# Strassen block products of four feed-forward stages: another order of weight roundings, sums and first pair on each engine, a fourth raw weight buffer, and rests at stretch ends on GpSimd

## The chip, the cores and the metric

The kernel runs on one core of a Trainium2 chip. The metric is the device time of one execution in microseconds (us). Engines are named as in the profile: PE is TensorE, DVE is VectorE, ACT is ScalarE, POOL is GpSimd, SP is SyncE (it issues the weight transfers).

## The reference

Two transformer layers with a context stream come first (neighbourhood attention, differential attention, a convolution branch), then two "macaron" layers on 512 positions of width 1024. Each of those has two feed-forward stages, so there are four:

```
def macaron_layer(x, mixer, ...):
    x = x + FFN_HALF * rmsnorm(swiglu(rmsnorm(x, ffn1_pre_g), ffn1_w_in, ffn1_w_out), ffn1_post_g)
    x = x + rmsnorm(mixer(rmsnorm(x, mix_pre_g)), mix_post_g)
    x = x + FFN_HALF * rmsnorm(swiglu(rmsnorm(x, ffn2_pre_g), ffn2_w_in, ffn2_w_out), ffn2_post_g)
    return x
```

`swiglu` multiplies by `w_in` (1024 by 5632: 2816 gate and 2816 up columns), takes silu(gate) * up, and multiplies by `w_out` (2816 by 1024). All is fp32.

## The kernel before

**Three products for one.** Every fp32 weight piece w is split into hi (rounded to the PE's fp32r format by ACT, line 390) and lo = w - hi (a subtraction on POOL or DVE, line 405 for whole pieces, 410 and 416 for others). The activations are split in the same way. PE then makes hi*hi + hi*lo + lo*hi (`mm3`).

**Units.** A feed-forward stage has 22 tiles of 128 hidden columns, each with a gate piece and an up piece of `w_in` (512 KB each). Tiles 0, 1 and 2 ("direct") are multiplied plainly. Each tile u from 3 to 21 is a *unit*: gate and up together are one 2 by 2 block product made with seven block products in Winograd's form of Strassen's scheme. The operands are quarters of the gate and up pieces ("plain"), four weight sums, and four combinations t0 to t3 of the activations. The weight sums are made by POOL: s1 and s2 (lines 425 and 427, together the entry "s12"), s3 and s4 (lines 429 and 431, "s34"). ACT rounds them (line 390), DVE makes their lo (line 416). The second half of the up piece is the entry "last" (lo at line 410 on DVE). A unit on PE is, in this order, the products p1, p2 (plain), p5, p6 (s12), then p4 of the unit before (its "last"), then p7, p3 (s34). Each product is 4 x 3 matmuls of 128x256, so a unit is 84.

**What is done with the products.** ACT copies p1 out of PSUM (line 1449); p6 of the same unit is added to the same bank, and so waits for that copy. ACT copies U2 = p1 + p6 (line 1456). DVE makes c11 (1582), u4 (1588), c22 (1597), c12 (1555, `gate_dve`) and c21 (1564, `up_dve`), scales gate and up by the norm (1502, twice), multiplies (1508), and makes the lo of the result (1513). ACT makes silu (1416) and the hi of the result (1423).

**Phases.** The units of a stage run in three stretches: 3 to 7, 8 to 15, 16 to 21. After each stretch the products with `w_out` follow (`ProjectOut`, 8 whole pieces). All orders on the engines are written out by hand in `Ffn.act`, `Ffn.dve`, `Ffn.pool`, `Ffn.pe`. Entries of weights are processed in the order of the list `ents`; `round_to` (ACT) and `rest_to` (DVE or POOL) work through it up to a limit.

**ACT in a unit u before:**

```
round plain(u+1); copy p1(u); silu(u-1); copy U2(u); round s12(u+1), last(u); hi of a(u-1); round s34(u+1)
```

**Buffers.** Raw pieces land in three buffers (`raw_sb`, `N_RAW` = 3). Piece n is fetched when piece n - 3 is free: a gate piece after the sum s4 (line 431) of its unit, an up piece after the lo of "last" (line 410), which for unit u stands in unit u+1 or late in unit u. SP issues all fetches in order (line 363). Split pieces (hi, lo) rotate through four pairs of buffers; "last" has a pair of its own.

**The start of a stage** ("direct"): four pieces are multiplied while the border with the stage before is finished (`HalfBorder`, `Border`), then two more. DVE makes t0 (1480), t1 and t2 (1484), t3 (1491); ACT rounds the four (1412), lo of t0 is made by DVE and lo of t1 to t3 by POOL (1497).

Of the kernel before, what the change touches and what calls it, by code (L numbers as in the profile page):

```python
# [57 lines left out]
DIRECT = 3  # L58
# [29 lines left out]
for _name, _n in (("ident", 128), ("ones", 128), ("head_ones", 128), ("rot", 128), ("eps", 2),  # L88
                  ("cos", 512), ("sin", 512), ("upper", 256), ("pick", 128),
                  ("suffix", 128), ("minus", 128)):  # L90
    CONSTS[_name] = (N_CONST, _n)
    N_CONST += _n
# [102 lines left out]
def build(nc, ins, out_dram):  # L195
# [6 lines left out]
    with ctx:  # L202
# [110 lines left out]
        ent_at = {ent: k for k, ent in enumerate(ents)}  # L313

# [32 lines left out]

        def raw_of(n):
            return raw_sb[n % N_RAW][:, 0:ins[order[n][0]].shape[-1]]
# [10 lines left out]
        def fetch_weights(q, e, n):  # L360
            if n >= N_RAW:
                q.wait_ge(*at("raw free", n - N_RAW))
            e.dma_start(raw_of(n), ins[order[n][0]][order[n][1]]).then_inc(*sig(f"raw{n % N_RAW}", "raw", n, by=16))
# [12 lines left out]
        def round_to(q, e, limit):  # L376

            while q.w <= limit:
                k = q.w
                q.w += 1  # L380
                m, kind = ents[k]
                hi, lo = split_bufs(m, kind)
                if kind in ("s12", "s34"):
                    q.wait_ge(*at("weight sums", m, kind))
                    src = sums_of(m, kind)
                else:
                    q.wait_ge(*at("raw", m + (kind == "last")))
                    slot_free(q, k)
                    src = raw_of(m + 1)[:, QUARTER:] if kind == "last" else raw_of(m)
                e.activation(hi, src, ACT.Copy).then_inc(*sig("w_rounded", "weights hi", m, kind))  # L390
# [4 lines left out]
        def rest_to(q, e, limit, dve=False):  # L395

            name = "w_split_dve" if dve else "w_split"
            while q.w <= limit:
# [4 lines left out]
                if kind == "whole" and dve == ("ffn" in order[m][0] or m in last_leads) or (kind == "plain" and not dve):  # L403
# [4 lines left out]
                if kind == "last" and dve:  # L408
# [377 lines left out]
        class HalfBorder:  # L786
# [6 lines left out]
            def act(self, q, e, after):  # L793
# [44 lines left out]
        class Border:  # L838
# [7 lines left out]
            def act(self, q, e, after):  # L846
# [4 lines left out]
                if self.unscaled:  # L851
# [4 lines left out]
                    self.norm.squares.root(q, e, 0)  # L856
                else:
# [398 lines left out]
        class Ffn:  # L1256
# [169 lines left out]
            def act(self, q, e):  # L1426
                for i in (0, 1):
                    self.t_hi_act(q, e, i)
                self.silu_act(q, e, 0)
                self.t_hi_act(q, e, 2)  # L1430
                self.silu_act(q, e, 1)
                round_to(q, e, self.ent(DIRECT, "s12"))
                self.a_hi_act(q, e, 0)
                self.a_hi_act(q, e, 1)
                self.silu_act(q, e, 2)
                self.t_hi_act(q, e, 3)
                round_to(q, e, self.ent(DIRECT, "s34"))
                self.a_hi_act(q, e, 2)
                for p, out in enumerate(self.outs):
                    units = self.units(p)  # L1440
                    for u in units:
                        unit_end = self.ent(u, "s34")
                        more = u < units[-1]
# [2769 lines left out]
```

## Time and profile before

| | |
|---|---|
| median of 3 runs | 3603.94 us (3603.62 to 3606.51) |
| the profiled execution's own time | 3605.75 us |
| its span, first to last instruction | 3603.9 us |
| mean granted TensorE clock | 0.933 of full |
| PE busy | 3179.4 us, 88% |
| DVE, ACT, POOL busy | 1992.3, 1383.3, 1316.0 us |

The span is that of one execution. PE is busy most of it, but a matmul at half clock counts as busy too, so the granted clock is read beside the busy share. The four feed-forward stages have 76 units in all.

### The profile page before, as it was taken

The page shows a single profiled execution, that of the slowest core. Times are in us where ns is not written, and L with a number is a line of the kernel's source. Part 1 is how long each engine was busy: PE and PEld are TensorE (multiplying, and loading weights), DVE is VectorE, ACT ScalarE, POOL GpSimd, SP SyncE. Part 2 cuts the span into 40 slices and gives each one's busy share as a digit, 9 for nine tenths or more (in the row PEclk, how much of TensorE's full clock was granted, in tenths as well). Part 3 has the DMA queues.
Part 4 walks back from the last instruction along what each step waited for, and adds up shares of the span by engine and source line. Part 5 has one row for each costly group of instructions (what it writes and reads, how often), then busy time and mean ns, then how long its engine had stood idle before and what let it go on. Part 6 is the DMA issues. An engine that isn't in the chain of part 4 may idle for free.

```text
span 3603.9 us, 50073 instructions
## 1 busy us (share of the span) xinstructions
PE 3179.4 (88%) x20476; PEld 2679.7 (74%) x20476; DVE 1992.3 (55%) x3148; ACT 1383.3 (38%) x2398; POOL 1316.0 (37%) x971
## 2 busy tenths in 40 slices
PE   6999999999997988998998798887888999979787
PEld 4877677777777777866777787877777885678776
DVE  2255483266747464675546645576455617474645
ACT  3331373342643333433444323353233417443323
POOL 2233323335245334263213442424424343353432
PEclk9999999999998999997779899898999999989998
DMA  5212202211021221230001212122121320112222
GB/s 222 88 65 106 93 1 66 94 50 55 19 75 64 81 100 65 77 105 30 8 2 65 80 62 99 64 83 83 70 88 66 98 94 12 53 40 90 77 84 75
DMA packets 74163, 256.73 MB, mean 71 GB/s; under 512 B 8016, under 2 KB 11216, under 8 KB 72784
## 3 DMA queue, kind: packets, MB, share of 16 engines
q1 hardware_dynamic: 73072, 248.82, 20.3%
q0 software_dynamic: 864, 4.72, 0.4%
q8 instruction: 162, 2.65, 0.3%
q14 instruction: 65, 0.53, 0.0%
HBM read 251.41 MB, written 2.10 MB: 70 GB/s over the span
## 4 chain that ended last, share of the span: by engine, by line
PE 61%; DVE 16%; POOL 7%; issue 6%; DMA 5%; ACT 5%; SPq 0%; ACTq 0%; DVEq 0%; POOLq 0%
PE banks L439 59%; DMA w_raw<-in_l_ffn_w_in 4%; DVE area L1502 2%; PE banks L448 2%; POOL w_lo L405 2%; ACT w_hi L390 1%; DVE w_lo L416 1%; DVE w_last L410 1%; DVE w_lo L405 1%; POOL area L1497 1%; POOL w_sum L431 1%; POOL w_sum L425 1%; DVE area L1508 1%; POOL w_sum L429 1%; POOL w_sum L427 1%
## 5 line engine op out<-in xcount | busy, mean ns | idle before, releaser
L439 PE MATMUL banks<-area,w_hi 128*128 128x256 f32 (+3 forms) x6892 | 1709.4, 339 | 215.3 <-ACT area L1449 126.2
L439 PEld LDWEIGHTS banks<-area,w_hi 128*128 128x128 f32 (+2 forms) x6892 | 1195.1, 194 | 396.4 <-ACT area L1449 134.8
L439 PE MATMUL banks<-area,w_lo 128*128 128x256 f32 (+3 forms) x3446 | 1150.7, 336 | 0.0
L405 POOL TENSOR_TENSOR w_lo<-w_raw,w_hi 128x1024 fp32r<-128x1024 f32 (+1 forms) x179 | 416.5, 2329 | 914.5 <-ACT w_hi L390 914.5
L439 PEld LDWEIGHTS banks<-area,w_lo 128*128 128x128 f32 (+2 forms) x3446 | 668.9, 194 | 69.7
L439 PE MATMUL banks<-area,w_late 128*128 128x256 f32 (+2 forms) x2766 | 510.5, 338 | 58.0 <-ACT area L1449 48.7
L439 PEld LDWEIGHTS banks<-area,w_late 128*128 128x128 f32 (+1 forms) x2766 | 428.5, 197 | 119.7 <-ACT area L1449 51.7
L390 ACT ACTIVATE w_hi<-w_raw 128x1024 fp32r<-128x1024 f32 (+2 forms) x271 | 269.5, 1001 | 568.2 <-PE banks L439 282.9
L439 PE MATMUL banks<-area,area 64*64 64x32 f32 (+11 forms) x4424 | 402.4, 316 | 66.3 <-DMA area<-in_w_mod 16.4
L439 PEld LDWEIGHTS banks<-area,area 64*64 64x64 f32 (+4 forms) x4424 | 309.4, 174 | 147.7 <-issue 57.6
L405 POOL TENSOR_TENSOR w_late<-w_raw,w_late 128x1024 fp32r<-128x1024 f32 (+1 forms) x45 | 110.6, 2458 | 324.1 <-ACT w_late L390 324.1
L439 PE MATMUL banks<-area,const 128*128 128x512 f32 (+7 forms) x566 | 162.3, 441 | 40.3 <-DVE area L1666 7.9
L416 DVE TENSOR_TENSOR w_lo<-w_sum,w_hi 128x1024 fp32r<-128x1024 f32 x115 | 152.4, 1326 | 63.8 <-POOL w_sum L431 63.8
L390 ACT ACTIVATE w_hi<-w_sum 128x1024 fp32r<-128x1024 f32 x115 | 121.4, 1056 | 171.9 <-POOL w_sum L427 126.8
L439 PE MATMUL banks<-area,w_last 128*128 128x256 f32 x912 | 161.4, 342 | 11.1 <-DVE area L1597 11.1
L439 PEld LDWEIGHTS banks<-area,w_last 128*128 128x128 f32 x912 | 156.2, 256 | 13.1 <-issue 13.1
L504 POOL TENSOR_TENSOR area<-area,area 128x512 f32<-128x512 f32 (+1 forms) x72 | 91.9, 1280 | 190.9 <-ACT area L489 188.9
L405 DVE TENSOR_TENSOR w_lo<-w_raw,w_hi 128x1024 fp32r<-128x1024 f32 (+1 forms) x92 | 112.7, 1233 | 72.6 <-ACT w_hi L390 72.6
L1502 DVE TENSOR_TENSOR area<-area,area 128x512 f32<-128x512 f32 x152 | 149.5, 984 | 5.2
L439 PEld LDWEIGHTS banks<-area,const 128*128 128x128 f32 (+4 forms) x566 | 78.9, 179 | 98.2 <-issue 44.1
L2377 DVE SCALAR_TENSOR_TENSOR area<-area,par,area 128x783 f32<-128x783 f32 (+1 forms) x120 | 149.2, 1303 | 0.0
L1186 DVE COPY area<-banks 128x512 f32<-128x512 f32 (+1 forms) x74 | 47.1, 645 | 181.1 <-PE banks L439 168.7
(286 smaller groups left out, 3708.4 us busy)
## 6 DMA issues: line engine op xcount, KB each, us to landing
w_raw<-in_l_ffn_w_in SPq DMA_DIRECT2D x176, 512.0 KB, 3.4
w_raw<-in_w_in SPq DMA_DIRECT2D x66, 512.0 KB, 3.6
w_raw<-in_l_ffn_w_out SPq DMA_DIRECT2D x64, 512.0 KB, 4.1
w_raw<-in_w_mod SPq DMA_DIRECT2D x32, 512.0 KB, 4.6
w_raw<-in_l_ffn_w_out SPq DMA_DIRECT2D x32, 384.0 KB, 3.1
w_raw<-in_w_qkv SPq DMA_DIRECT2D x24, 512.0 KB, 3.3
w_raw<-in_l_w_in SPq DMA_DIRECT2D x22, 512.0 KB, 3.3
w_raw<-in_w_out SPq DMA_DIRECT2D x32, 320.0 KB, 2.9
```

What stands on the lines that cost most here:

```text
L390: e.activation(hi, src, ACT.Copy).then_inc(*sig("w_rounded", "weights hi", m, kind))
L405: e.tensor_tensor(lo, raw_of(m), hi.bitcast(f32), SUB).then_inc(*sig(name, "weights", m, kind))
L410: e.tensor_tensor(lo, raw_of(m + 1)[:, QUARTER:], hi.bitcast(f32), SUB).then_inc(*sig(name, "weights", m, kind))
L416: e.tensor_tensor(lo, sums_of(m, kind), hi.bitcast(f32), SUB).then_inc(*sig(name, "weights", m, kind))
L425: e.tensor_tensor(s1, u0, u1, ADD).then_inc(*sig("w_sums"))
L427: e.tensor_tensor(s2, s1, g0, SUB).then_inc(*sig("w_sums", "weight sums", m, kind))
L439: return e.matmul(out, lhsT, rhs, start=first, stop=stop, skip_group_check=True)
L448: return e.transpose(out, in_, ident[0:k, 0:k])
L504: e.tensor_tensor(a, a, self.slot_of(s, j)[:, 0:c1 - c0], ADD).then_inc(*sig("squares_added", *self.tag, "added", s, j))
L1186: e.tensor_copy(yy, b).then_inc(*sig("evicted_dve", "evicted", u))
L1502: e.tensor_tensor(v, v, self.norm.rs, MUL).then_inc(*sig("ffn_scaled"))
L2377: e.scalar_tensor_tensor(yy, uu, w, yy, MUL, ADD).then_inc(*sig("taps", self.tag, "tap", m, k))
```

## The change

- **List of entries**: plain(u), last(u-1), s12(u), s34(u) in place of plain(u), s12(u), last(u-1), s34(u). At the end of a stretch: s34, whole `w_out` piece 0, last, whole piece 1.
- **ACT in a unit**: copy p1(u); round plain(u+1); round s34(u); silu(u-1); copy U2(u); round last(u), s12(u+1); hi of a(u-1).
- **DVE in a unit**: the lo of s34(u) between c11 and u4 of the same unit; after c22 the lo of last(u) and of s12(u+1), then the lo of a(u-1).
- **POOL**: s4 before s3 (DVE may overwrite the s12 buffer after s4).
- **A fourth raw buffer** from the first piece of the first feed-forward stage on. It lies over the cos and sin tables, which are moved to the front of `const`; its first fetch waits for their last use in the second layer.
- **Rests at stretch ends**: the lo of `w_out` piece 0, of last, and of `w_out` piece 1 (`end_ents`) go from DVE to POOL.
- **Direct part**: ACT rounds t0 already in the border; DVE makes lo of t0, then t3, then lo of t1 (on POOL before), then lo of s12 and s34 of unit 3, and only then the scalings and products of tiles 0 and 1; tile 2 is taken into unit 3 (`third_dve`). POOL makes lo of t2, then the work of unit 4, then lo of t3.

```
-for _name, _n in (("ident", 128), ..., ("cos", 512), ("sin", 512), ("upper", 256), ("pick", 128),
+for _name, _n in (("cos", 512), ("sin", 512), ("ident", 128), ..., ("upper", 256), ("pick", 128),
...
-                    ents += [(n, "plain"), (n, "s12")]
-                    if ents[-3][1] == "s34":
-                        ents.append((ents[-3][0], "last"))
-                    ents.append((n, "s34"))
-                elif order[n + 1][0] != name:
-                    ents.append((n - 1, "last"))
+                    ents.append((n, "plain"))
+                    if ents[-2][1] == "s34":
+                        ents.append((ents[-2][0], "last"))
+                    ents += [(n, "s12"), (n, "s34")]
             elif split:
+                after_units = len(ents) > 0 and ents[-1][1] == "s34"
                 ents.append((n, "whole"))
+                if after_units:
+                    ents.append((ents[-2][0], "last"))
+        end_ents = {k + i for k, (n, kind) in enumerate(ents) if kind == "s34" and ents[k + 1][1] == "whole" for i in (1, 2, 3)}
...
+        over_angles = piece_no["l0_ffn1_w_in", 0]
+        raw_sb.append(const)
+        raw_slots, last_raw = [], [None] * N_RAW
+        for n in range(len(order)):
+            if n == over_angles:
+                last_raw.append(None)
+            oldest = min(range(len(last_raw)), key=lambda i: (last_raw[i] is not None, last_raw[i] or 0, i))
+            raw_slots.append((oldest, last_raw[oldest]))
+            last_raw[oldest] = n
...
         def fetch_weights(q, e, n):
-            if n >= N_RAW:
-                q.wait_ge(*at("raw free", n - N_RAW))
+            slot, before = raw_slots[n]
+            if before is not None:
+                q.wait_ge(*at("raw free", before))
+            elif slot == N_RAW:
+                q.wait_ge(*at(layer1.late.tag, "q", "cos", 3))
+                q.wait_ge(*at(layer1.late.tag, "q", "sin", 3))
...
-                if kind == "whole" and dve == ("ffn" in order[m][0] or m in last_leads) or (kind == "plain" and not dve):
+                if (kind == "whole" and dve == (("ffn" in order[m][0] or m in last_leads) and k not in end_ents)
+                        or (kind == "plain" and not dve)):
...
-                if kind == "last" and dve:
+                if kind == "last" and dve == (k not in end_ents):
...
                 if kind in ("s12", "s34") and dve:
-                    q.wait_ge(*at("weight sums", m, "s34"))
+                    q.wait_ge(*at("fourth sum", m))
...
-                        e.tensor_tensor(s3, g0, u0, SUB).then_inc(*sig("w_sums"))
                         q.wait_ge(*at("weight sums", m, "s12"))
-                        e.tensor_tensor(s4, g1, s2, SUB).then_inc(*sig("w_sums", "weight sums", m, kind))
+                        e.tensor_tensor(s4, g1, s2, SUB).then_inc(*sig("w_sums", "fourth sum", m))
+                        e.tensor_tensor(s3, g0, u0, SUB).then_inc(*sig("w_sums", "weight sums", m, kind))
...
+                    after.t_hi_act(q, e, 0)
                 norm.squares.root(q, e, 0)
...
             def act(self, q, e):
...
+                self.t_hi_act(q, e, 1)
+                round_to(q, e, self.ent(DIRECT, "s12"))
                 self.t_hi_act(q, e, 2)
+                round_to(q, e, self.ent(DIRECT, "s34") + 1)
                 for p, out in enumerate(self.outs):
                     for u in units:
-                        if more:
-                            round_to(q, e, unit_end + 1)
                         q.wait_ge(*at(self.tag, "product", u, "p1"))
...
+                        if u == DIRECT:
+                            for v in (0, 1):
+                                self.silu_act(q, e, v)
+                        else:
+                            round_one(q, e, unit_end + 1)
+                            if q.w <= unit_end:
+                                round_one(q, e, unit_end)
+                            q.w = unit_end + 2
                         if u > units[0]:
                             self.silu_act(q, e, u - 1)
...
-                        round_to(q, e, unit_end + (3 if more else 1))
+                        if u == DIRECT:
+                            for v in (0, 1):
+                                self.a_hi_act(q, e, v)
+                            self.t_hi_act(q, e, 3)
+                        round_to(q, e, unit_end + 3)
...
-                        round_to(q, e, unit_end + (4 if more else 3))
...
             def direct_dve(self, q, e):
                 self.combined_dve(q, e)
+                self.t_lo_dve(q, e, 0)
+                self.last_combined_dve(q, e)
+                self.t_lo_dve(q, e, 1)
+                rest_to(q, e, self.ent(DIRECT, "s34"), dve=True)
                 self.norm.scaled(q)
...
+            def third_dve(self, q, e):
+                ... (gate of tile 2 from PSUM, lo of a(0), up of tile 2 from PSUM, lo of a(1))
...
             def dve(self, q, e):
...
                             *sig("ffn_quarter", self.tag, "c11", u))
+                        rest_to(q, e, unit_end, dve=True)
...
-                        if not more:
-                            rest_to(q, e, unit_end + 1, dve=True)
+                        if u == DIRECT:
+                            self.third_dve(q, e)
...
-                        rest_to(q, e, unit_end + (3 if more else 2), dve=True)
+                        rest_to(q, e, unit_end + 3, dve=True)
...
-                        rest_to(q, e, unit_end + (4 if more else 3), dve=True)
+                        elif u == DIRECT:
+                            self.product_dve(q, e, 2)
+                            self.a_lo_dve(q, e, 2)
...
             def pool(self, q, e):
                 rest_to(q, e, self.ent(DIRECT, "s34"))
-                for i in (1, 2, 3):
-                    self.t_lo_dve(q, e, i, "t_lo_pool")
+                self.t_lo_dve(q, e, 2, "t_lo_pool")
+                rest_to(q, e, self.ent(DIRECT + 1, "s34"))
+                self.t_lo_dve(q, e, 3, "t_lo_pool")
                 for p, out in enumerate(self.outs):
-                    rest_to(q, e, self.ent(self.units(p)[-1], "last"))
+                    rest_to(q, e, self.ent(self.units(p)[-1], "last") + 1)
                     out.pool(q, e)
```

## Rows read from the trace of the kernel before

**Rows 1.** The page: busy time and share of the span by engine.
```profile
PE 3179.4 (88%) x20476; PEld 2679.7 (74%) x20476; DVE 1992.3 (55%) x3148; ACT 1383.3 (38%) x2398; POOL 1316.0 (37%) x971
```

**Rows 2.** Waits of PE over the span: us in total, times, longest.
```profile
PE banks L439 <- ACT area L1449: 174.8, 56, 3.9
PE banks L439 <- DVE w_lo L416: 41.5, 7, 9.9
PE banks L439 <- POOL w_lo L405: 16.4, 6, 4.5
...
PE banks L439 <- DVE area L1597: 11.1, 12, 0.9
```

**Rows 3.** Windows: start:end, us; busy PE, PEld, DVE, ACT, POOL; PEclk; DMA share; GB/s.
```profile
1106.39:1162.89 56.50, 45.11 (x303) 44.12 (x304) 32.62 (x42) 19.47 (x30) 32.06 (x21) 0.81 0.16 57
1222.10:1321.73 99.63, 79.54 (x586) 78.34 (x585) 56.83 (x76) 35.72 (x53) 54.34 (x35) 0.88 0.19 64
1380.18:1449.40 69.22, 57.05 (x411) 56.24 (x409) 37.44 (x52) 24.91 (x38) 37.72 (x25) 0.85 0.17 61
1250.90:1266.00 15.10, 11.43 (x84) 11.22 (x84) 9.42 (x12) 5.32 (x9) 7.86 (x5) 0.89 0.20 73
1180.50:1220.60 40.10, 40.10 (x172) 32.25 (x173) 14.11 (x15) 8.49 (x9) 7.53 (x5) 1.00 0.27 92
```

**Rows 4.** Timeline of one unit: start, us, engine, line, idle before and releaser.
```profile
1249.89 1.06 ACT L390 ACTIVATE w_late<-w_raw 128x1024 fp32r<-128x1024 f32 x1 [4.03 <-DMA w_raw<-in_l_ffn_w_in]
1250.86 0.37 ACT L1449 ACTIVATE area<-banks 128x256 f32<-128x256 f32 x1
1251.03 2.37 POOL L405 TENSOR_TENSOR w_late<-w_raw,w_late 128x1024 fp32r<-128x1024 f32 x1 [7.34 <-ACT w_late L390]
...
1251.27 0.80 PE L439 MATMUL banks<-area,w_hi 128*128 128x256 f32 x2 [3.61 <-ACT area L1449]
1251.31 0.42 DVE L1582 TENSOR_TENSOR area<-banks,area 128x256 f32<-128x256 f32 x1 [2.20 <-ACT area L1449]
```

**Rows 5.** SP's waits, 1222 to 1322 us.
```profile
SPq L363 <- DVE w_last L410: 83.1, 6, 14.4
```

**Rows 6.** Timeline of one unit where DVE and POOL meet, and PE beside them.
```profile
1237.89 2.75 PE L439 MATMUL banks<-area,w_last 128*128 128x256 f32 x12
...
1240.45 3.01 PE L439 MATMUL banks<-area,w_late 128*128 128x256 f32 x24
...
1240.70 1.29 POOL L429 TENSOR_TENSOR w_sum<-w_raw 128x512 f32<-128x512 f32 x1
...
1241.14 1.41 DVE L1502 TENSOR_TENSOR area<-area,area 128x512 f32<-128x512 f32 x1
...
1241.96 1.73 POOL L431 TENSOR_TENSOR w_sum<-w_raw,w_sum 128x512 f32<-128x512 f32 x1
1242.58 1.66 DVE L1508 TENSOR_TENSOR area<-area,area 128x512 f32<-128x512 f32 x1
```

**Rows 7.** Two lines of DVE: duration in ns, min/median/max.
```profile
L1502 DVE TENSOR_TENSOR area<-area,area x152: 691/693/1815, 1119.3 to 3553.6; 128x512 f32<-128x512 f32 x152
L416 DVE TENSOR_TENSOR w_lo<-w_sum,w_hi x115: 1207/1215/3375, 1099.3 to 3541.5; 128x1024 fp32r<-128x1024 f32 x115
```

**Rows 8.** Timeline of the start of the third feed-forward stage: DVE, then POOL, then PE.
```profile
2417.04 7.30 DVE L1484 SCALAR_TENSOR_TENSOR area<-x_lat,par,area 128x256 f32<-128x256 f32 x8
...
2437.88 3.38 DVE L416 TENSOR_TENSOR w_late<-w_sum,w_late 128x1024 fp32r<-128x1024 f32 x1
...
2430.82 9.35 POOL L1497 TENSOR_TENSOR area<-area,area 128x1024 fp32r<-128x1024 f32 x3 [8.35 <-DVE area L1491]
2440.14 3.37 POOL L405 TENSOR_TENSOR w_lo<-w_raw,w_hi 128x1024 fp32r<-128x1024 f32 x1
...
2435.24 0.79 PE L439 MATMUL banks<-area,w_hi 128*128 128x256 f32 x2 [9.90 <-DVE w_lo L416]
...
2455.54 0.73 PE L439 MATMUL banks<-area,w_hi 128*128 128x256 f32 x2 [3.35 <-ACT area L1449]
```

More of the change, by code:

```diff
@@ L87 @@
 CONSTS, N_CONST = {}, 0
-for _name, _n in (("ident", 128), ("ones", 128), ("head_ones", 128), ("rot", 128), ("eps", 2),
-                  ("cos", 512), ("sin", 512), ("upper", 256), ("pick", 128),
+for _name, _n in (("cos", 512), ("sin", 512), ("ident", 128), ("ones", 128), ("head_ones", 128), ("rot", 128), ("eps", 2),
+                  ("upper", 256), ("pick", 128),
                   ("suffix", 128), ("minus", 128)):
@@ L346, in ahead @@
             return min(first_ent[n] + more, len(ents) - 1)
+        over_angles = piece_no["l0_ffn1_w_in", 0]
[7 more added lines that the diff above has]
+            last_raw[oldest] = n
         def raw_of(n):
-            return raw_sb[n % N_RAW][:, 0:ins[order[n][0]].shape[-1]]
+            return raw_sb[raw_slots[n][0]][:, 0:ins[order[n][0]].shape[-1]]
         def split_bufs(n, kind="whole"):
@@ L360, in fetch_weights @@
         def fetch_weights(q, e, n):
-            if n >= N_RAW:
-                q.wait_ge(*at("raw free", n - N_RAW))
-            e.dma_start(raw_of(n), ins[order[n][0]][order[n][1]]).then_inc(*sig(f"raw{n % N_RAW}", "raw", n, by=16))
+            slot, before = raw_slots[n]
[4 more added lines that the diff above has]
+                q.wait_ge(*at(layer1.late.tag, "q", "sin", 3))
+            e.dma_start(raw_of(n), ins[order[n][0]][order[n][1]]).then_inc(*sig(f"raw{slot}", "raw", n, by=16))
         def slot_free(q, k):
@@ L378, in round_to, with round_one @@
             while q.w <= limit:
-                k = q.w
                 q.w += 1
[L381 to L390, printed above, removed]
+                round_one(q, e, q.w - 1)
+        def round_one(q, e, k):
+            m, kind = ents[k]
+            hi, lo = split_bufs(m, kind)
+            if kind in ("s12", "s34"):
+                q.wait_ge(*at("weight sums", m, kind))
+                src = sums_of(m, kind)
+            else:
+                q.wait_ge(*at("raw", m + (kind == "last")))
+                slot_free(q, k)
+                src = raw_of(m + 1)[:, QUARTER:] if kind == "last" else raw_of(m)
+            e.activation(hi, src, ACT.Copy).then_inc(*sig("w_rounded", "weights hi", m, kind))
         def rest_of_weights(q, e, n, more=None, dve=False):
@@ L856, in act @@
                     self.norm.squares.root(q, e, 0)
+                    after.t_hi_act(q, e, 0)
                 else:
@@ L1442, in act @@
                         unit_end = self.ent(u, "s34")
-                        more = u < units[-1]
-                        if more:
-                            round_to(q, e, unit_end + 1)
                         q.wait_ge(*at(self.tag, "product", u, "p1"))
@@ L1450, in act @@
                             *sig("ffn_p1", self.tag, "p1", u))
+                        if u == DIRECT:
+                            for v in (0, 1):
+                                self.silu_act(q, e, v)
+                        else:
+                            round_one(q, e, unit_end + 1)
+                            if q.w <= unit_end:
+                                round_one(q, e, unit_end)
+                            q.w = unit_end + 2
                         if u > units[0]:
@@ L1532, in direct_dve @@
                     self.product_dve(q, e, u)
-                self.last_combined_dve(q, e)
-                for u in (0, 1):
-                    self.a_lo_dve(q, e, u)
+            def third_dve(self, q, e):
                 q.wait_ge(*at("projected", self.project.group(4, 0)))
@@ L1540, in direct_dve @@
                 also(self.tag, "gate", 2)
-                rest_to(q, e, self.ent(DIRECT, "s12"), dve=True)
+                self.a_lo_dve(q, e, 0)
                 q.wait_ge(*at("projected", self.project.group(5, 0)))
@@ L1546, in direct_dve @@
                 also(self.tag, "scaled", 2)
-                self.product_dve(q, e, 2)
-                rest_to(q, e, self.ent(DIRECT, "s34"), dve=True)
-                self.a_lo_dve(q, e, 2)
+                self.a_lo_dve(q, e, 1)
             def gate_dve(self, q, e, u):
@@ L1577, in dve @@
                             self.gate_dve(q, e, u - 1)
-                        more = u < units[-1]
                         q.wait_ge(*at(self.tag, "product", u, "p2"))
@@ L1589, in dve @@
                             *sig("ffn_u4", self.tag, "u4", u))
-                        if not more:
-                            rest_to(q, e, unit_end + 1, dve=True)
+                        if u == DIRECT:
+                            self.third_dve(q, e)
                         if u > units[0]:
```

15 lines of the change are left out of this document (3 added, 12 removed).

## The prediction

> **What bounds the kernel now.** I read the busy shares first [rows 1]: PE is busy 88% of the span, so the question is what the other 12%, and the part of the 88% that runs at half clock, wait for. The list of PE's waits answers it [rows 2]: the largest by far is 174.8 us, 56 times, for line 1449, the ACT copy of p1. That is 3.1 us in nearly every unit. Next come 41.5 us for the lo of the weight sums (four of these waits are the 9 to 10 us at the starts of the stages), 16.4 us for a lo on POOL, and about 2.5 us at each of the 12 stretch ends, the first 0.9 of it on line 1597.
>
> The windows [rows 3] give the price of a unit: the first three run from one p1 copy to another, the fourth is one ordinary unit, the fifth a run of `w_out` products. From the copy of p1 in unit 3 to that in unit 7 there are 4 intervals in 56.50 us; in the second stretch 7 intervals in 99.63; in the third 5 in 69.22: 16 intervals in 225.35 us, 14.1 on average, with 15.1 for an ordinary one. (The other three feed-forward stages repeat this within 1 us a stretch.) The clock in these stretches is 0.81 to 0.88; in a `w_out` run, where PE never idles, it is 1.00. At full clock 24 matmuls take 3.01 us and at half clock 12 take 2.75 [rows 6], so a unit's 84 matmuls cost 10 to 10.5 us by those rows (they overlap their neighbours; start to start I reckon 9.8). The rest of the 15.1 is 3.1 of standing and some 2 of half clock behind it.
>
> The timeline shows who is late [rows 4]. ACT sat 4.03 us until a gate piece landed, rounded it, and only then copied p1, which had been ready for 3 us; PE went on 0.05 us behind the copy. So the wait is the weight transfer's, not ACT's. And the transfer was late because its queue waited for the lo of "last" (line 410), 83.1 us in six units [rows 5]: with three raw buffers the next gate piece can't be fetched until the up piece of two units ago is done with.
>
> **The change, part by part.**
>
> *Order on ACT and the fourth raw buffer.* Both take this wait away. p1 is copied before the rounding of plain(u+1), and with four buffers the fetch of gate(u+1) is released by the sums of unit u-1, almost a unit before it is needed. If nothing else took its place, a unit would cost 9.8 to 10.4 us.
>
> *What is late next.* DVE and POOL. In a timeline where they meet [rows 6], DVE's L1502, which takes 0.69 us alone [rows 7], takes 1.41: it began inside POOL's L429 and ended 0.56 us behind that one's end. POOL's L431, 1.29 alone, then took 1.73, and DVE's L1508 ended 0.55 behind it. The same holds for a long pair [rows 8]: L416 took 3.38, and POOL's L405 behind it 3.37 instead of the 2.37 of [rows 4]. But L1582, with one operand in PSUM, ran 0.42 in the middle of an L405 [rows 4]. So an operation of DVE with both operands in SBUF and one of POOL never run together, and at a boundary they take turns. A half-width DVE operation costs POOL 0.44 us, a full one 0.99.
>
> Per unit POOL has L405 (2.38) and four sums (4 x 1.29 [rows 6]) = 7.5 us. DVE has five half-width operations (two scalings, product, lo of a, lo of last) and two full ones (lo of s12, of s34). 7.5 + 5 x 0.44 + 2 x 0.99 = 11.7 us. That is the new floor of a unit, above PE's 9.8.
>
> I laid out two units in the new order, with these prices, from the start of p1(u) at 0 and products of 1.4 us. p1 copied at 1.9, plain(u+1) rounded at 2.95, L405 from 3.05 to 5.4; the lo of s34(u), rounded at 4.0, must wait for it and ends at 6.45, in time for p7 at 7.0. The sums follow with one DVE operation at each boundary and end at 12.95, so the lo of s12(u+1) ends at 14.05: p5(u+1), which PE reaches at 12.6, waits 1.5 us. In unit u+1, L405 begins at 13.95, in front of the lo of a, the scaling and the lo of s34(u+1), which ends at 20.85 where PE wants it at 18.35: 2.6 us of waiting. p5(u+2) starts at 26.6 without a wait. So 23.8 us for two units, 11.9 each.
>
> The stalls of 1.5 and 2.6 us can still halve the clock for a while: a wait of 3.61 did so at once [rows 4]. If PE is slow behind the longer one, p1(u+2) ends 1.5 us later, and its copy, the rounding of the next plain piece and POOL move with it: 25.4 for two, 12.7 each. I take 12.4. Bounds: below, 11.7 less a little overlap, 11.6; above, 13.4, where a DVE operation bars POOL for its whole 0.69 or 1.22 us (7.5 + 5 x 0.69 + 2 x 1.22).
>
> The Trainium skill (SBUF — State Buffer, "SBUF: two separate sides") says that VectorE and GpSimd share a port pair as an exclusive lock for the whole instruction, and counts operations with two SBUF inputs among those that take it. The exclusion is as in the trace; held for whole durations it would give the 13.4 above and a total near 3556, while the 0.44 measured in the trace gives the 11.7.
>
> Sum: 225.35 - 16 x 12.4 = 27.0 us a stage, x 4 = 108 us.
>
> *Lo of s34 within its own unit, s4 before s3.* No instruction added. It is in the layout above; its cover is the 4 us between the rounding and p7.
>
> *Direct part.* DVE's line of work up to the lo of s12(3), for which PE waited until 2435.24 [rows 8], loses eight short operations and the gate of tile 2 (nine starts, some 0.61 apart, 5.5 us), but gains the lo of t1 (1.2). t1 and t2 are done at 2424.34 as before (2417.04 + 7.30 [rows 8]); lo of t0, t3 and lo of t1, unhindered, would put the lo of s12(3) at 2429.5. But ACT (three roundings of 1.05 behind t1) now lets POOL start lo of t2 at about 2426, and L405 and sums of unit 4 follow, so from there each DVE operation waits for one of POOL: by hand the lo of s12(3) ends at 2436.4, 1.2 later than before. The deferred work comes back in unit 3, but the three lo of t on POOL (9.35 us [rows 8]) no longer stand in front of unit 4's sums. p5(4) comes out at 2448.3 by hand, against 2450.8 before (PE stood 3.35 until 2455.54 [rows 8], and p5 is the 1.4 in front), which is the saving of an ordinary interval already counted. I take 0. Bounds: -5 us a stage if DVE keeps ahead of POOL (the 2429.5), +1 the other way.
>
> *Stretch ends.* Three lo go to POOL, where a whole one takes 2.37 for DVE's 1.22. They stand in front of the c22 on which PE waits there (line 1597, 11.1 us in 12 times [rows 2]), and of two further waits like it. DVE gets c22 done earlier, POOL ends later: 0, bounds -15 and +14 (12 ends x 1.2).
>
> *Fourth buffer in the mixers.* POOL's late lo (16.4 us [rows 2]) are behind late pieces in part: -4, bounds 0 and -12. The wait for the cos and sin tables is long over when the first such fetch comes up. The extra rounding of t0 ahead of the norm's root (1.05 us) delays only scalings that now come later.
>
> Total: 3605.75 (own time) - 108 - 4 = 3494; the median of the runs is 1.8 lower: **3492 us**.
>
> **Rivals.**
>
> 1. *PE is the bound*, units of about 10.4: the DVE and POOL operations fit beside each other. 225.35 - 166 = 59 x 4 = 236 less: 3365. Against it is every meeting of the two in [rows 6, 8]. 0.08 for anything under 3420.
> 2. *The stall only moves*: p5 and p7 wait about as long as p6 did, and the clock stays at 0.85. DVE, ACT and POOL each work in a fixed order, so one late operation can hold up two others. Units of 13.6 on average: 3605 - 4 x 7.7 = 3574. For it: DVE misses a boundary whenever it stands at a wait for PE (c22, u4). 0.08 for 3560 to 3597.
> 3. *Slower, because the rounding of s34(u) now stands behind that of plain(u+1)*. If gate(u+1) lands late, p7(u) waits for two roundings, L405 and the lo: 1.06 + 1.06 + 2.4 + 1.1 less overlap = 4.6 us behind the landing, where p6 before waited 1.4. PE wants p7 5.6 us behind the end of p1, so the loss starts when the piece lands 1.0 behind p1's end and outweighs the gain at 2.7. If it slipped by a whole fetch (3.4 us) beyond the 1.0, a unit would cost 15.8: + 64 x 1.7 = 3715. Against it: two fetches of 3.4 fill half of a unit, and both are released a unit early. 0.07.
> 4. *Nothing changes within 0.2%* (7 us, about what this measurement can tell from no change): only if 2 and something of 3 cancel. 0.03.
>
> The forecast, 3420 to 3560, has 0.74. The range takes in units of 11.7 to 13.4 and the bounds of the other parts: 3492 - 45 - 20 - 7 at the low end, 3492 + 64 + 4 at the high end (the ends' bounds of 15 and 14 are as likely to go against a unit's as with it, and are left out of both). Faster by over 0.2%: 0.74 + 0.08 + 0.08 = 0.90; within: 0.03; slower: 0.07.
>
> **What would show it.** In the profile after, waits of PE on line 1449 should be almost gone, and waits on lines 416 (p5 and p7) should take their place with 2 us or less a unit. An ordinary interval between p1 copies should be 11.7 to 12.8. The mean of L1502, L1508, L1513 and L416 should rise (1.0 to 1.3 us for the short ones), and POOL's durations by 0.4 to 1.0 where DVE got in; POOL should be busy over 75% of a unit, with PE's clock at 0.9 or higher. SP should wait for line 410 without ACT waiting for the DMA. The first wait for L416 in each stage should stay near 10 us. The prediction is wrong if DVE's short operations keep 0.69 us within POOL's, if ACT still idles on the transfer, or if the direct part moves by more than 5 us a stage.

## The result: faster by 4%, and the profile after

The changed kernel takes 3462.20 us (median of 4, 3456.78 to 3468.37) against 3605.23 before on the same chips: 0.960 of before, 95% interval 0.9579 to 0.9621. The forecast was 3492 in a range of 3420 to 3560. The profiled execution took 3456.78, its span is 3455.0, so 148.9 us less than the span before.

The waits of PE over the span, to be read against [rows 2] (line 459 is `mm`, 436 the lo of the weight sums, 1624 c22, 1460 the copy of p1):

```profile
PE banks L459 <- DVE w_lo L436: 120.7, 67, 10.4
PE banks L459 <- DVE w_late L436: 29.3, 24, 2.6
PE banks L459 <- DVE area L1624: 16.6, 12, 2.5
PE banks L459 <- POOL w_lo L425: 16.1, 6, 4.5
```

The 174.8 us behind the copy of p1 have gone altogether. In their place stand 150 us for the lo of the weight sums, of which 41 are the four waits of 9.5 to 10.4 us at the starts of the stages. Windows from one p1 copy to the next, five units of the second stretch of the first stage (columns as in [rows 3]):

```profile
1221.67:1233.29 11.62, 10.42 (x86) 10.01 (x85) 11.52 (x11) 5.51 (x8) 10.89 (x6) 1.00 0.24 81
1233.29:1246.24 12.95, 10.37 (x86) 9.96 (x85) 12.85 (x14) 5.28 (x9) 9.60 (x5) 1.00 0.23 82
1246.24:1257.40 11.16, 10.10 (x86) 9.90 (x85) 11.06 (x12) 5.51 (x8) 9.52 (x5) 1.00 0.27 96
1257.40:1270.36 12.96, 10.37 (x86) 9.96 (x85) 12.86 (x14) 5.28 (x9) 9.37 (x5) 1.00 0.23 82
1270.36:1281.53 11.17, 10.10 (x86) 9.89 (x85) 11.07 (x12) 5.51 (x8) 9.53 (x5) 1.00 0.27 95
```

The reader is to see three things. A unit that took 15.1 us takes 12.95 and 11.16 in turns, 12.06 on average. These are the shortest pairs: over the 16 ordinary pairs of the four stages (starts of line 1460, without the first two intervals and the unpaired last one of a stretch) two units take 24.1 to 25.5 us, 12.35 a unit on average. DVE shows as busy 99% of the time, though its own work is only 8 us; the rest is waiting inside its instructions. And the clock is 1.00, against 0.89 in the unit of [rows 3]. Where DVE's time goes, and how PE waits before p7, stands in the timeline of one such unit (one row of ACT, then DVE, POOL and PE; start, duration, instruction, and in brackets the idle time before it with what ended it):

```profile
1246.24 0.39 ACT L1460 ACTIVATE area<-banks 128x256 f32<-128x256 f32 x1 [0.49 <-PE banks L459]
...
1248.12 2.48 DVE L1528 TENSOR_TENSOR area<-area,area 128x512 f32<-128x512 f32 x1
1250.52 0.41 DVE L1608 TENSOR_TENSOR area<-banks,area 128x256 f32<-128x256 f32 x1
1250.86 1.98 DVE L436 TENSOR_TENSOR w_lo<-w_sum,w_hi 128x1024 fp32r<-128x1024 f32 x1
...
1247.65 2.40 POOL L425 TENSOR_TENSOR w_lo<-const,w_hi 128x1024 fp32r<-128x1024 f32 x1 [3.12 <-PE banks L459]
1250.01 1.74 POOL L445 TENSOR_TENSOR w_sum<-w_raw 128x512 f32<-128x512 f32 x1
1251.83 2.15 POOL L447 TENSOR_TENSOR w_sum<-w_sum,const 128x512 f32<-128x512 f32 x1
...
1241.73 0.50 PE L459 MATMUL banks<-area,w_hi 128*128 128x256 f32 x2 [2.22 <-DVE w_lo L436]
...
1250.24 1.59 PE L459 MATMUL banks<-area,w_last 128*128 128x256 f32 x12
1252.89 0.50 PE L459 MATMUL banks<-area,w_hi 128*128 128x256 f32 x2 [1.06 <-DVE w_lo L436]
...
1259.13 3.07 PE L459 MATMUL banks<-area,w_late 128*128 128x256 f32 x24 [0.37 <-DVE w_late L436]
```

ACT now idles before the copy of p1 and waits for PE; it does not idle for the transfer. The scaling L1528 takes 2.48 us in place of 0.69, because it began inside the L425 and ended 0.55 behind its end (1250.05). L445 (1.29 alone) took 1.74 behind it, L436 ended 1.09 behind L445, and L447 took 2.15. That is the alternation of [rows 6]. The PE rows of 1241.73 and 1252.89 both follow a p4 (the `w_last` row), so both are the start of p7: it waits 2.22 and 1.06 us in turns. Only one p5 of each pair waits, 0.37 us (the last row).

The end of a stretch is where something was lost. DVE, POOL and PE at the end of the first stretch:

```profile
1162.05 2.75 DVE L1534 TENSOR_TENSOR area<-area,area 128x512 f32<-128x512 f32 x1
1164.72 0.41 DVE L1624 TENSOR_TENSOR area<-banks,area 128x256 f32<-128x256 f32 x1
...
1161.43 2.82 POOL L425 TENSOR_TENSOR w_late<-w_raw,w_late 128x1024 fp32r<-128x1024 f32 x1
...
1165.28 1.66 PE L459 MATMUL banks<-area,w_last 128*128 128x256 f32 x12 [2.03 <-DVE area L1624]
```

The product L1534 (0.68 alone) stands behind POOL's lo of a `w_out` piece and ends 0.55 behind it, at 1164.80. Behind it comes c22 (L1624), for which the last p4 waits: PE stands 2.03 us, where it stood 0.92 before. This wait is 2.0 to 2.5 us at six of the eight ends of the first two stretches, and 0.57 us at the other two and at the four ends of the third. What got better is that the two waits behind it (0.8 us for the lo of a `w_out` piece, 0.8 for the lo of a) are gone at the eight ends of the first two stretches. All of PE's waits at the 12 ends (from 9 us before the first `w_out` product to 15 behind it) sum to 32.9 us before and 24.1 after.

To see where the 148.9 us came from, I cut each trace at the first and last 512-column matmuls around the units. "5 units" is from the end of the directly multiplied tiles to the first product with `w_out`; the means of the four stages, in us, with the kernels tried below:

| | 5 units | 8 units | 6 units | `w_out` between | all else, in sum |
|---|---|---|---|---|---|
| before | 84.1 | 112.0 | 81.2 | 46.1, 46.1 | 2125.6 |
| after | 77.1 | 97.0 | 70.4 | 45.0, 45.3 | 2116.1 |
| fourth buffer alone | 74.8 | 94.4 | 69.3 | 46.1, 46.1 | 2134.9 |
| new orders, three buffers | 78.6 | 101.4 | 73.9 | 45.6, 45.4 | 2129.0 |
| rests on DVE | 74.7 | 95.8 | 71.1 | 45.0, 45.0 | 2123.0 |
| rests on DVE, old start | 74.5 | 94.5 | 70.7 | 45.0, 45.0 | 2126.8 |
| lo of plain on DVE | 70.8 | 90.5 | 66.7 | 45.0, 45.0 | 2119.4 |

So the units gave 4 x (7.0 + 15.0 + 10.8) = 131 us, the `w_out` runs 4 x 1.9 = 8, all else 9. That last column moves by up to 10 us between executions of kernels that are equal there, so no cause is read from it.

### The profile page after: what moved, and what is told of

It is laid out like the page before. It is cut to its first block, busy times and chain, and to the rows that moved or that the text cites. A ratio compares the mean times of both kernels' runs of the same rounds, so it can differ in the third digit from the quotient of the medians.

```text
span 3455.0 us, 50031 instructions
## 1 busy us (share of the span) xinstructions
PE 3112.0 (90%) x20476; PEld 2613.2 (76%) x20476; DVE 2193.9 (63%) x3116; ACT 1379.3 (40%) x2398; POOL 1493.2 (43%) x1003
## 4 chain that ended last, share of the span: by engine, by line
PE 66%; DVE 19%; issue 5%; ACT 4%; POOL 4%; DMA 1%; SPq 0%; ACTq 0%; DVEq 0%; POOLq 0%
PE banks L459 64%; DVE area L1539 3%; DVE w_lo L436 3%; PE banks L468 2%; POOL w_lo L425 1%; ACT w_hi L409 1%; DVE area L1510 1%; POOL w_sum L447 1%; DVE area L1528 1%; DVE w_late L436 1%; DVE w_last L430 1%; DVE area L1517 1%; POOL w_sum L445 1%; DMA area<-in_w_mod 1%; DVE area L1534 0%
## 5 line engine op out<-in xcount | busy, mean ns | idle before, releaser
L459 PE MATMUL banks<-area,w_hi 128*128 128x256 f32 (+3 forms) x6892 | 1690.8, 337 | 154.1 <-DVE w_lo L436 120.7
L459 PEld LDWEIGHTS banks<-area,w_hi 128*128 128x128 f32 (+2 forms) x6892 | 1179.8, 191 | 335.4 <-DVE w_lo L436 134.3
L425 POOL TENSOR_TENSOR w_lo<-w_raw,w_hi 128x1024 fp32r<-128x1024 f32 (+2 forms) x146 | 344.8, 2363 | 517.1 <-ACT w_hi L409 479.5
L409 ACT ACTIVATE w_hi<-w_raw 128x1024 fp32r<-128x1024 f32 (+2 forms) x197 | 193.2, 985 | 321.3 <-PE banks L459 199.7
L436 DVE TENSOR_TENSOR w_lo<-w_sum,w_hi 128x1024 fp32r<-128x1024 f32 x115 | 207.1, 1803 | 47.1 <-POOL w_sum L450 42.4
L425 POOL TENSOR_TENSOR w_late<-w_raw,w_late 128x1024 fp32r<-128x1024 f32 (+2 forms) x47 | 117.1, 2491 | 223.5 <-ACT w_late L409 197.3
L425 POOL TENSOR_TENSOR w_lo<-const,w_hi 128x1024 fp32r<-128x1024 f32 (+1 forms) x50 | 130.7, 2614 | 171.3 <-ACT w_hi L409 112.7
L1528 DVE TENSOR_TENSOR area<-area,area 128x512 f32<-128x512 f32 x152 | 168.0, 1105 | 5.3
L1539 DVE TENSOR_TENSOR area<-area,area 128x512 fp32r<-128x512 f32 x88 | 137.7, 1565 | 15.5 <-ACT area L1445 15.5
L1438 ACT ACTIVATE area<-area 128x512 f32<-128x512 f32 x88 | 55.2, 628 | 219.1 <-DVE area L1528 186.0
```

What stands on the lines that cost most here:

```text
L425: e.tensor_tensor(lo, raw_of(m), hi.bitcast(f32), SUB).then_inc(*sig(name, "weights", m, kind))
L459: return e.matmul(out, lhsT, rhs, start=first, stop=stop, skip_group_check=True)
L1438: e.activation(self.sg[u % 2], self.sg[u % 2], ACT.Silu).then_inc(*sig("ffn_silu", self.tag, "silu", u))
L1528: e.tensor_tensor(v, v, self.norm.rs, MUL).then_inc(*sig("ffn_scaled"))
L1539: e.tensor_tensor(self.a_lo[:, k, :], self.a[u % 2], self.a_hi[:, k, :].bitcast(f32), SUB).then_inc(*sig("a_split", self.tag, "a", u))
```

## The experiments

Every kernel is timed against the kernel before on its chip. The changed kernel was run again with the last of them; that is the first entry, since it says how far the others can be compared.

**The changed kernel again.** 

> The changed kernel once more, unchanged, beside the two others on their chip, to see how far runs of different calls can be compared: 0.960 of before within 0.002.

3467.94 us, 0.961 (0.9596 to 0.9625). Differences of 0.002 between groups of runs are not read as effects. The times before differ by chip (3605 to 3612 us), so the ratios are compared first.

**The fourth raw buffer alone**, on the kernel before:

```
+        raw_sb.append(const)       # and cos, sin first in const
+            if n == over_angles:
+                last_raw.append(None)
...
         (every order on ACT, DVE, POOL as before)
```

> The kernel before with the fourth raw weight buffer alone; all orders on the engines stay as before. Theory 1 (the 3.1 us that PE stands for the copy of p1 are the late transfer's, and DVE and POOL, which exclude each other, are the next floor): ACT's idle time on the transfer goes, and units fall from 15.1 to 12.8 to 13.5 us, because here POOL's next L405 must wait for two roundings of ACT behind its last sum (2 x 1.06). About 3530 us, 70 less than before. Rival (the order on ACT is what holds p1 up, the buffer is spare): within 10 us of before.

3461.48 us, 0.9575 (0.9557 to 0.9594). One buffer gives all that the whole change gives, and perhaps 0.2% more. The 3530 expected was 70 us too long, and the rival fell. ACT's, DVE's and POOL's rows in a unit of it:

```profile
1249.67 1.05 ACT L404 ACTIVATE w_hi<-const 128x1024 fp32r<-128x1024 f32 x1
1250.62 0.37 ACT L1463 ACTIVATE area<-banks 128x256 f32<-128x256 f32 x1
...
1260.71 1.06 ACT L404 ACTIVATE w_hi<-w_sum 128x1024 fp32r<-128x1024 f32 x1 [0.52 <-POOL w_sum L445]
1261.68 1.05 ACT L404 ACTIVATE w_hi<-w_raw 128x1024 fp32r<-128x1024 f32 x1
...
1260.71 1.23 DVE L430 TENSOR_TENSOR w_late<-w_sum,w_late 128x1024 fp32r<-128x1024 f32 x1 [0.85 <-POOL w_sum L445]
1261.86 0.68 DVE L424 TENSOR_TENSOR w_last<-w_raw,w_last 128x512 fp32r<-128x512 f32 x1
1262.46 0.69 DVE L1527 TENSOR_TENSOR area<-area,area 128x512 fp32r<-128x512 f32 x1
...
1250.80 3.43 POOL L419 TENSOR_TENSOR w_lo<-const,w_hi 128x1024 fp32r<-128x1024 f32 x1 [3.19 <-ACT w_hi L404]
1262.80 2.61 POOL L419 TENSOR_TENSOR w_lo<-w_raw,w_hi 128x1024 fp32r<-128x1024 f32 x1 [2.12 <-ACT w_hi L404]
```

The old order is there (rounding first, then the copy of p1, line 1463), and it costs nothing once the piece has landed. The mechanism that I gave for a smaller gain is there too: POOL stands idle 2.1 to 3.2 us behind two roundings. But DVE uses this gap for its own SBUF operations, mostly without meeting POOL (the three DVE rows: the lo of s12, of last and of a). The units come out at 12.0 to 12.8 us and not at 12.8 to 13.5. That this is because the shared time is the same is my reading of the rows, not a test. What PE waits for most inside these units is another thing, u4 (line 1602 here): 50.7 us in 41 waits, where the changed kernel waits for the lo of the sums.

**The new orders with three raw buffers:**

```
-            if n == over_angles:
-                last_raw.append(None)
```

> The changed kernel with three raw buffers again; all its orders stay. Theory 1: gate(u+1) is released by the lo of last(u-1), lands some 3.4 us into unit u, plain(u+1) is rounded 1.5 us later than now, and since POOL and DVE together are the floor, each unit loses 1.2 to 1.5 us: 3540 us, waits of PE on the lo of the sums longer, none on the copy of p1. Rival (the order alone did it): 3462 us, as the changed kernel.

3502.87 us, 0.9697 (0.9682 to 0.9713). Both theories miss. The orders by themselves bring 3%, because p1 is copied ahead of the late piece; the buffer's absence costs 1.0% and not 2.2. ACT's waits from 1240 to 1310 us:

```profile
ACT w_hi L407 <- POOL w_sum L445: 15.1, 5, 3.4
ACT w_hi L407 <- DMA w_raw<-in_l_ffn_w_in: 10.4, 3, 3.6
ACT w_late L407 <- DMA w_raw<-in_l_ffn_w_in: 6.8, 2, 3.5
```

ACT still stands 3.4 us a unit for the piece, but p1 is copied ahead of it; what comes late behind it is POOL's lo of plain (L423 here). Ordinary units are 13.0 us, 0.65 more than the 12.35 with four buffers. So each of the two measures covers most of what the other does, and they don't add.

**POOL held back at the start of a stage:**

```
                 self.t_lo_dve(q, e, 2, "t_lo_pool")
+                q.wait_ge(*at("weights", self.piece(DIRECT), "s12"))
                 rest_to(q, e, self.ent(DIRECT + 1, "s34"))
```

> The changed kernel, with one more wait on POOL at the start of each feed-forward stage: the work of unit 4 begins only when DVE has made the lo of s12 of unit 3. The 10.4 us for which PE stands there should shrink to about 5 in any case. Theory 1 (up to unit 4 the start is one line of work on DVE, which is never idle there, so a shorter PE stall is paid back behind it): 0 to 8 us less in all, 3454 to 3462. Rival (PE's stall is the price): 4 x 5 us less, 3442.

3467.10 us, 0.9599 (0.9585 to 0.9614): the same as the changed kernel. PE's waits from 1040 to 1160 us in it:

```profile
PE banks L459 <- DVE w_lo L436: 9.9, 4, 5.5
PE banks L459 <- DVE area L1615: 5.3, 1, 5.3
```

The long wait fell from 9.5 to 5.5 us (from 10.4 to 6.4 in the other stages), and a new one of 5.3 came up behind it, for u4 (line 1615), which DVE reaches no earlier. That fits the start as one line of work on DVE; the PE stall isn't its price.

**The rests at stretch ends back on DVE:**

```
-        end_ents = {k + i for k, ... if kind == "s34" and ents[k + 1][1] == "whole" for i in (1, 2, 3)}
+        end_ents = set()
```

> The changed kernel, with the lo of the two first pieces of the output product and of last at the stretch ends back on DVE. As predicted, this part is worth 0 with bounds of 15 us: 3462 within 8 us. Rival 1: DVE is the full engine at the stretch ends too, so giving it 3.1 us of work back costs up to 12 x 1.5 = 18 us. Rival 2: POOL's lo takes twice as long and stood in front of the output product, so this is 10 us faster.

3449.24 us, 0.9543 (0.9528 to 0.9557). This part of the change costs 0.57%, some 20 us with an error of 9; the kernel with POOL held back, timed beside it, is 18 us slower. So it is a loss, but whether it is more than my bound of 14 is not settled. Rival 2 is right in the direction. On DVE the same three take 3.1 us where it has time:

```profile
1305.68 1.22 DVE L425 TENSOR_TENSOR w_lo<-const,w_hi 128x1024 fp32r<-128x1024 f32 x1
1306.81 0.68 DVE L430 TENSOR_TENSOR w_last<-w_raw,w_last 128x512 fp32r<-128x512 f32 x1
1307.41 1.22 DVE L425 TENSOR_TENSOR w_late<-w_raw,w_late 128x1024 fp32r<-128x1024 f32 x1
...
1307.55 1.70 PE L459 MATMUL banks<-area,w_last 128*128 128x256 f32 x12 [1.24 <-DVE w_last L430]
```

c22 stands in front of them again and is never late; the last p4 now waits 1.0 to 1.2 us for the lo of last instead. PE's waits at the 12 ends sum to 15.9 us, against 24.1 in the changed kernel (26.4 in its second trace). That is 8 to 10 us of the loss. The rest is not placed: the ordinary units are as long as before, and the table has 12 us less in the units, nearly all in the first two stretches and none in the third.

**The old start of a stage**, on top of that: `t_hi_act(0)` out of the borders, the first lines of `Ffn.act`, `direct_dve` and `Ffn.pool` as in the kernel before, without `third_dve`:

```
+                for i in (1, 2, 3):
+                    self.t_lo_dve(q, e, i, "t_lo_pool")
...
-                        if u == DIRECT:
-                            self.third_dve(q, e)
```

> As the run with the rests at stretch ends on DVE (3449 us, 0.9543 of before), with the start of each stage as before the change: t0 rounded behind the border, lo of t1 to t3 on POOL, tiles 0 to 2 finished ahead of unit 3. Theory 1 (as predicted: DVE's line of work to the lo of s12(4) is the same in sum, the part is worth 0): within 8 us of 3449. Rival A (the profile after says that PE still stands 10.4 us there and the first five units took 77.1 us where the kernel with only the fourth buffer takes 74.8): 4 x 2.3 = 9 us faster, 3440. Rival B (the new start is worth its trouble): 10 us or more slower.

3443.06 us, 0.9542 (0.9526 to 0.9558), as the run before it. The reordering of the start is worth 0.

**One more operation on POOL in each unit:**

```
+                        e.tensor_tensor(s3, g0, u0, SUB).then_inc(*sig("w_sums"))
+                        q.wait_ge(*last())
                         e.tensor_tensor(s3, g0, u0, SUB).then_inc(*sig("w_sums", "weight sums", m, kind))
```

> The changed kernel with the sum s3 made twice on POOL in each of the 76 units (one more operation of 1.29 us, waiting for the first; the output is not changed). POOL is busy some 75% of a unit. Theory 1 (POOL and the SBUF operations of DVE exclude each other, and their sum is a unit's floor): units of 12.1 become 13.4, in 64 to 76 units 83 to 100 us more, about 3550. Rival A (DVE's own line of work is the floor, POOL has a quarter of its time to spare): at most 15 us more. Rival B (PE's waits for the chain through ACT): at most 15 us more.

3528.33 us, 0.9774 (0.976 to 0.9789). By the ratios that is 59 to 63 us more (66 by the times), some 0.8 for each of 76 units, for an engine that idled a fifth of the unit: both rivals (at most 15) fall. It is less than the 83 to 100 of the theory. The first two intervals of the second and third stretches keep their 8.4 and 11.6 us, so they have room; the ordinary pairs, such as 15.6 and 11.4, average 13.3 a unit, 0.95 more than 12.35.

**One more operation with a PSUM operand on DVE in each unit:**

```
+                        e.tensor_tensor(self.u4[u % 2], self.quarter(u, 2), self.u2[u % 2], ADD).then_inc(
+                            *sig("ffn_u4"))
+                        q.wait_ge(*last())
```

> The changed kernel with u4 made twice on DVE in each of the 76 units (one more operation of 0.42 us with an operand in PSUM, which does not exclude POOL; the output is not changed). DVE shows as busy 99% of a unit. Theory 1 (that busy time holds the waits for POOL; the floor is the shared time): the operation hides under a POOL operation, 0 to 10 us more. Rival A (DVE's line is the floor): 76 x 0.45 = 34 us more.

3480.68 us, 0.9644 (0.9628 to 0.966). That is 12 to 16 us over the changed kernel by the ratios, between hidden (0 to 10) and full price (34), so the time alone doesn't decide. The traces do for the ordinary units. Their 16 pairs average 12.5 us a unit, against 12.35 to 12.4 in the two traces of the changed kernel: an operation of 0.42 us costs 0.1 to 0.15 there, so it hides for the most part. The third stretch has much of the rest: cut as for the table, its 6 units take 73.1 us in place of 70.4, and at three of its four ends PE waits 2.45 us for c22 instead of 0.57.

**The lo of the plain gate piece on DVE**, with the rests on DVE too. A fetch into a gate's buffer then also waits for that lo:

```
-                        or (kind == "plain" and not dve)):
+                        or (kind == "plain" and dve == (m in plain_dve))):     # units 4 to 21
...
                             *sig("ffn_u4", self.tag, "u4", u))
+                        rest_to(q, e, unit_end + 1, dve=True)
```

> As the run with the rests at stretch ends on DVE, and the lo of the plain gate piece of units 4 to 21 is made by DVE (1.22 us, behind u4) and not by POOL (2.38 us). Theory 1: the shared time of a unit falls from 11.7 (7.5 + 5 x 0.44 + 2 x 0.99) to 10.3 (5.2 + 5 x 0.44 + 3 x 0.99), units from 12.1 to 11.2 or so: about 3395. Rival A (DVE's line is the floor): 1.14 us more in each of 72 units, 3449 + 82 = 3531.

3392.45 us, 0.9403 (0.9389 to 0.9417), against 3395 forecast. The window over four of its units, and POOL's waits in it:

```profile
1237.52:1283.94 46.42, 40.42 (x338) 39.62 (x338) 43.89 (x53) 22.04 (x33) 28.26 (x17) 1.00 0.27 92
```

```profile
POOL w_sum L449 <- DMA w_raw<-in_l_ffn_w_in: 17.3, 4, 4.4
```

A unit is 11.6 us, where the theory said 11.2 or so, so that the total is met to 3 us is in part luck. DVE has one operation more and is busy less (43.89 of 46.42), for it stands less within POOL's. The next wait shows as well: POOL stands 4.3 us a unit for the up piece, whose buffer is freed by the lo of last. Whether this is what keeps the unit at 11.6, above the 10.3 of shared time, was not tested.

**The same in every second unit:**

```
+        plain_dve = {n for n, kind in ents if kind == "plain" and order[n][1] > 2 * DIRECT and order[n][1] // 2 % 2}
```

> As the run with the lo of the plain gate piece on DVE, but in every second unit only. Theory 1: half of its gain, about 3422. Rival A: half of its loss, 3490. If DVE's line and the shared time lie close to each other, this one is the fastest of the three, since DVE has 8.0 us of its own work in a unit with the piece on POOL and 9.2 with it.

3412.51 us, 0.9459 (0.9445 to 0.9473): between the two, with more than half of the gain (37 of 57 us, or 0.84 of 1.40%). DVE's line is not the tighter limit.

**The fastest: the lo of plain on DVE, the rests on DVE, the old start.**

> As the run with the lo of the plain gate piece on DVE (3392 us, 0.9403 of before), with the start of each stage as before the change. If the two starts are equal, 3392; by rival A of the run before 3383; by rival B over 3402. With DVE's line fuller here (it makes the lo of plain as well), the three lo of t on POOL should help a little more: I expect 3385.

3389.09 us, 0.9397 (0.9383 to 0.9411), within 0.1% of the run with the new start and 4 us over the 3385 expected. It beats both kernels, the changed one, timed beside it, by 2.3%; nothing of that is shown to be due to the start.

## Why the prediction was right, point by point

*What bounded the kernel: right.* The copy of p1 waited for the transfer, and with it gone ACT waits for PE. Shown twice: by the buffer alone, and by the orders alone.

*"Both take this wait away": true, but I did not ask what each would do alone.* I priced order and buffer as one. The buffer alone gives 0.9575, the orders alone 0.9697, both with the rests left on DVE 0.9542. The orders' share on top of the buffer is 0.3%, hardly more than the error of the two ratios (0.24%).

*What is late next: right, and this decided the number.* The exclusion of DVE's SBUF operations and POOL's gave a floor of 11.7 us and a layout of two units, 23.8 us long without the clock and 25.4 with it; I took 12.4 a unit. The 16 ordinary pairs take 24.1 to 25.5 us, 12.35 a unit. Where the waits fall I had half right: 1.5 at p5 and 2.6 at p7 were laid out, 0.37 at p5 and 1.06 and 2.22 at p7 were measured, 3.65 in place of 4.1 for the pair. Two tests bear the exclusion out: 1.29 us more on POOL cost some 60 us, and 2.38 moved off POOL for 1.22 on DVE brought 51 to 57, with 54 forecast. Rival 1 (PE is the bound, 3365) fell; rivals 2 and 3 fell too.

The Trainium skill (SBUF — State Buffer, "SBUF: two separate sides") has the lock held for the whole instruction. The trace agrees that the later one is held up: L1528 ended 0.55 us behind L425. It does not agree that the price is the whole instruction, since 0.14 of DVE's 0.69 lay inside POOL's, and POOL's L445 behind it lost only 0.45.

*The allowance for half clock: right for the ordinary unit.* I raised 11.9 to 12.4, with a pair at 25.4 where PE is slow. The shortest pairs, 24.11 us, ran at 1.00. The third and fourth interval of each stage's first stretch are such a slow pair, and elsewhere the slow pairs lie between; the windows of one pair from the first stretch and one from another:

```profile
1126.76:1142.36 15.60, 11.92 (x86) 11.52 (x85) 15.49 (x16) 5.39 (x8) 12.11 (x7) 0.89 0.26 80
1142.36:1152.19 9.83, 9.83 (x86) 9.83 (x85) 8.45 (x10) 5.40 (x8) 8.20 (x5) 1.00 0.23 90
2076.89:2091.62 14.73, 11.92 (x86) 11.52 (x85) 14.63 (x16) 5.28 (x9) 9.20 (x6) 0.88 0.27 85
2091.62:2101.44 9.82, 9.82 (x86) 9.82 (x85) 8.43 (x10) 5.39 (x8) 8.19 (x5) 1.00 0.24 90
```

The first pair is 25.43 us, the second 24.56. PE runs the next unit without a wait and makes part of the loss up.

*The sum, 16 x 12.4 a stage: this is the term that was mis-sized.* It forecast 27.0 us a stage; the cut of the traces gives 32.8 for the units, so it is short by 23 us in all, most of the 30 by which the forecast is too long. By stretches the forecast was 6.9, 12.8 and 7.2 us, and 7.0, 15.0 and 10.8 were measured, so all of it lies in the second and third. There I charged the price of an ordinary unit for every interval. The first interval of these stretches takes 8.4 to 8.5 us and the second 11.6 to 11.7, so the two cost 4.7 us less than 24.8. In the first PE never stands:

```profile
1213.19:1221.67 8.48, 8.48 (x74) 8.48 (x73) 2.49 (x5) 3.31 (x6) 6.84 (x5) 1.00 0.07 14
```

The first unit has no p4 of a unit before, and its sums are made while PE still runs the `w_out` products (in the trace POOL makes them from 1200.7 to 1208.8 us). The last interval of these stretches, which is the long one of a pair with no short one behind it, takes 14.1 on average and so gives 1.7 us of this back.

*The direct part, 0: right.* The first wait stayed at 9.5 to 10.4 us. The old start on the same kernel is equal (0.9542 and 0.9543).

*Stretch ends, 0 with bounds of -15 and +14: wrong.* The part cost some 20 us, at the edge of the bound. The step that failed is "DVE gets c22 done earlier": POOL's lo bars DVE's product, which stands in front of c22, and c22 came 2.0 to 2.5 us late at six ends, where it had been 0.92 late before. The Trainium skill (GPSIMD Engine Reference, "When to use GPSIMD") sends elementwise work with two inputs to VectorE; the two changes that moved such work back agree, by some 20 and 51 to 57 us.

*Fourth buffer in the mixers, -4: nothing came of it.* POOL's late lo stand at 16.1 us in six waits, as before (16.4).

*Not forecast:* the `w_out` runs are 1.1 and 0.8 us shorter, 8 us in all. They are as long as before in the kernel with the buffer alone, where PE still waits 0.8 us for the lo of a some 6 us into the run; in the changed kernel that wait is gone at these ends. So the new orders are the cause; which of their steps was not tried.

## What to carry to other kernels

When one wait is taken away, lay out by hand a whole period of every engine that stands behind it, with the prices that they have when they meet; here that gave the ordinary unit (12.4 forecast, 12.35 measured). Then lay out the first units of a stretch too, which start with their pieces ready: here the two first intervals of a stretch cost 4.7 us less than two ordinary ones, and that I hadn't counted. Ask of each part of a change what it does without the others: a buffer and an order that both cure the same wait do not add. And where an engine's busy time grows without more work, look for the other engine that it stands in, and move work to whichever holds the shared thing for the shorter time, even if it already looks full.

## What the runs showed of the hardware

DVE at 99% busy was not full. After one more operation of 1.22 us a unit it was busy 95%, in a unit of 11.6 us instead of 12.35 on average, since POOL had 2.38 less. And a PE wait of 2.2 us at p7 was followed by half clock in some units and not in others with the same instructions. One case of either kind, by what followed:

```profile
1136.31 4.28 PE L459 MATMUL banks<-area,w_late 128*128 128x256 f32 x24 [2.20 <-DVE w_late L436]
...
1244.64 2.96 PE L459 MATMUL banks<-area,w_late 128*128 128x256 f32 x24
```

The 24 matmuls of p7 and p3 behind the wait of 2.20 us took 4.28, and the clock of the interval was 0.89. Those behind the wait of 2.22 began at 1241.73 (shown with the result), and the next product began 2.91 us later, at 1244.64; the clock was 1.00. What decides between the two stays open. The pairs with the slower clock were 0.4 to 1.4 us longer than 24.11.
